# Hybrid DiT backbone with PEER experts, 1 core: the second one-hot of the gate phase is compared by GpSimd ahead of time and comes back from DRAM

## The reference

```python
def peer(h, w_q, subkeys, u, v):                       # per block of 128 tokens
    q = (xb @ w_q).reshape(PEER_BLOCK, PEER_HEADS, 2, PEER_QDIM // 2)
    s = jnp.einsum('thpd,hpkd->thpk', q, subkeys)
    s1, i1 = lax.top_k(s[:, :, 0], PEER_TOPK)          # 16 of 128 keys
    s2, i2 = lax.top_k(s[:, :, 1], PEER_TOPK)
    cand = s1[..., :, None] + s2[..., None, :]
    cidx = i1[..., :, None] * PEER_KEYS + i2[..., None, :]
    sc, pos = lax.top_k(cand, PEER_TOPK)               # 16 experts a head, 8 heads
    idx = jnp.take_along_axis(cidx, pos, axis=-1)
    g = jax.nn.softmax(sc, axis=-1)
    act = jax.nn.gelu(jnp.einsum('thkd,td->thk', u[idx], xb))
    return jnp.einsum('thk,thkd->td', g * act, v[idx])
```

## Time and profile before

| | |
|---|---|
| median of 3 runs | 3708.85 us (3705.79 to 3709.24) |
| span of the profiled execution | 3700.4 us (its own time is not on the page) |
| TensorE busy | 3558.4 us, 96% |
| VectorE busy | 2666.9 us, 72% |
| ScalarE busy | 2003.8 us, 54% |
| GpSimd busy | 139.6 us, 4% |
| moved by DMA | 568.38 MB, mean 154 GB/s |

### The profile page before, as it was taken

How to read it: one execution, slowest core, us unless ns; L and a number is a source line. 1 busy time by engine, 2 the same in 40 slices (tenths; PEclk the granted TensorE clock), 3 DMA queues, 4 the chain that set the end, 5 groups by cost and what they waited for, 6 DMA issues and landing times.

```text
span 3700.4 us, 61292 instructions
## 1 busy us (share of the span) xinstructions
PE 3558.4 (96%) x22710; PEld 3113.8 (84%) x22710; DVE 2666.9 (72%) x5607; ACT 2003.8 (54%) x3922; POOL 139.6 (4%) x134
## 2 busy tenths in 40 slices
PE   7999999999998999999999999999899999979999
PEld 5877787888887899999998888888698888878888
DVE  5447733699868688888767776774765899686666
ACT  3345522566668555555557544434454666684444
POOL 0002000000012000000002000000100000030000
PEclk9999999999999999999999999999999999999999
DMA  5213222455645566566655566633044566605665
GB/s 206 82 67 138 94 97 83 144 183 182 186 151 159 167 187 184 185 186 184 187 184 152 161 186 198 195 119 111 9 164 136 176 187 182 187 29 165 188 190 172
DMA packets 142313, 568.38 MB, mean 154 GB/s; under 512 B 15920, under 2 KB 17456, under 8 KB 130352
## 3 DMA queue, kind: packets, MB, share of 16 engines
q1 hardware_dynamic: 142128, 566.16, 49.0%
HBM read 565.05 MB, written 1.05 MB: 153 GB/s over the span
## 4 chain that ended last, share of the span: by engine, by line
PE 82%; DVE 12%; ACT 3%; issue 2%; DMA 1%; POOL 1%; SPq 0%; DVEq 0%; POOLq 0%; ACTq 0%
PE ps L584 52%; PE ps L1081 13%; PE ps L1099 10%; PE ps L1083 6%; DVE low L1835 3%; DVE arena L1835 3%; ACT arena L1283 2%; DMA ring<-wmod_in 1%; POOL arena L2619 1%; DVE hot_found L1835 1%; DVE arena L2387 1%; DVE arena L2378 1%; DVE ring_low L1835 0%; DVE arena L2380 0%; DVE arena L2375 0%
## 5 line engine op out<-in xcount | busy, mean ns | idle before, releaser
L1283 ACT ACTIVATE high<-ring 128x512 fp32r<-128x512 f32 x1632 | 1028.4, 632 | 1014.7 <-PE ps L584 502.2
L1835 DVE TENSOR_TENSOR low<-ring,high 128x512 fp32r<-128x512 f32 x1632 | 1078.1, 690 | 290.4 <-ACT high L1283 279.4
L584 PE MATMUL ps<-h_pair,high 128*128 128x512 f32 x3456 | 1236.7, 398 | 17.6 <-DVE h_pair L1835 10.3
L584 PE MATMUL ps<-h_pair,low 128*128 128x256 f32 x3456 | 979.7, 283 | 0.0
L584 PEld LDWEIGHTS ps<-h_pair,high 128*128 128x128 f32 x3456 | 653.6, 189 | 171.1 <-issue 11.9
L1081 PE MATMUL ps<-wt,high 128*128 128x512 f32 x2016 | 706.3, 397 | 5.7 <-DVE low L1835 5.7
L584 PEld LDWEIGHTS ps<-h_pair,low 128*128 128x128 f32 x3456 | 655.0, 190 | 0.0
L1083 PE MATMUL ps<-wt,low 128*128 128x256 f32 x2016 | 562.4, 279 | 0.0
L1283 ACT ACTIVATE arena<-ps 128x256 f32<-128x256 f32 (+2 forms) x659 | 274.8, 427 | 382.3 <-PE ps L584 334.0
L1081 PEld LDWEIGHTS ps<-wt,high 128*128 128x128 f32 x2016 | 379.1, 188 | 97.2 <-issue 3.0
L584 PE MATMUL ps<-arena 128*128 128x128 f32 (+7 forms) x2536 | 355.1, 311 | 56.5 <-ACT arena L1283 44.2
(11 more groups left out here) (202 smaller groups left out, 4296.5 us busy)
## 6 DMA issues: line engine op xcount, KB each, us to landing
ring<-u_in SPq DMA_DIRECT2D x384, 512.0 KB, 3.6
ring<-v_in SPq DMA_DIRECT2D x384, 512.0 KB, 3.6
ring<-win_in SPq DMA_DIRECT2D x54, 1024.0 KB, 4.9
ring<-wmod_in SPq DMA_DIRECT2D x24, 1024.0 KB, 5.0
ring<-wq_in SPq DMA_DIRECT2D x48, 512.0 KB, 3.6
ring<-wmod_in SPq DMA_DIRECT2D x48, 512.0 KB, 3.7
ring<-wbr_in SPq DMA_DIRECT2D x16, 768.0 KB, 4.3
ring<-wout_in SPq DMA_DIRECT2D x8, 1024.0 KB, 4.9
```

What stands on the lines that cost most here:

```text
L584: return pe.matmul(o, l_, r, start=first, stop=last)
L1283: return act.activation(o, i_, f, **kw_)
L1835: return dve.tensor_tensor(o, a, b, op)
```

## The change

The second one-hot is no longer compared by VectorE in the gate phase. GpSimd compares it in the u stage, token by token, as soon as the routing result of a half is copied: 32 groups of 8 instructions of 128 x 128, in bfloat16, into four buffers (`hot2_made`). SyncE stores each group to DRAM (`keep_hot2`, 256 KB): groups 0 to 15 after the loads of chunks 66, 68, ... 96, groups 16 to 31 after those of 112 to 127. In the gate phase SyncE loads them back (`bring_hot2`), at most three in flight, into two plus four buffers, of which the four lie over `high`. ScalarE widens from there. Of the eight tokens of a group GpSimd now multiplies six and ScalarE two. `hot2_made` lies over `hot1`, so the first gated copies wait until the last store is done. In layer 1 four chunks of v are loaded between the loads of groups 4 and 5; in layer 0 each modulation chunk is loaded behind a group's one-hot. The second index is copied to float32 (`RT[:, 1]`) where it was bfloat16 (`route2`).

```diff
@@ sync: new functions
+            def keep_hot2(pp, g):
+                sp.wait_ge(*at("ssd_xd", "hot2_made", pp, g))
+                if g:
+                    sp.wait_ge(*at("stored", "hot2", pp, g - 1))
+                sp.dma_start(hot2_kept[pp][g], hot2_made[:, g % 4, :]).then_inc(*inc("stored", "hot2", pp, g, by=16))
+
+            def bring_hot2(pp, g):
+                sp.wait_ge(*at("stored", "hot2", pp, g))
+                if g >= 3:
+                    sp.wait_ge(*at(hot2_loaded(g), "hot2", pp, g - 3))
+                if g >= 6:
+                    sp.wait_ge(*at("hot2", pp, g - 4))
+                elif g >= 2:
+                    sp.wait_ge(cnt.sem("half_free"), 2 * PN["u", pp, CHUNKS - 1] + 2)
+                sp.dma_start(hot2_in(g), hot2_kept[pp][g]).then_inc(*inc(hot2_loaded(g), "hot2", pp, g, by=16))
@@ sync: u stage and gate phase
                         chunk(("u", pp, c))
-                    if l + 1 < DEPTH:
-                        for n in range(2 * MOD_PASS):
-                            chunk(("m", pp, n))
+                        if c in STORE_AT:
+                            keep_hot2(pp, STORE_AT.index(c))
+                    for g in range(5):
+                        bring_hot2(pp, g)
+                    v_ahead = 0 if l + 1 < DEPTH else 4
+                    for c in range(v_ahead):
+                        chunk(("v", pp, c))
+                    for g in range(5, GROUPS):
+                        bring_hot2(pp, g)
+                        if l + 1 < DEPTH and g - 5 < 2 * MOD_PASS:
+                            chunk(("m", pp, g - 5))
@@ scalar: gate_hot1
                     if g >= 2:
                         act.wait_ge(*at("g_product", pp, g - 2))
-                    for j in range(GROUP // 2, GROUP):
+                    else:
+                        act.wait_ge(*at("stored", "hot2", pp, GROUPS - 1))
+                    for j in range(3 * GROUP // 4, GROUP):
...
-                    act.wait_ge(*at("hot2_found", pp, g))
-                    fn(hot2[:, g % 2, :, :].rearrange("p (a b) k -> p a b k", b=2),
-                       hot2_found[:, g % 2, :, :].rearrange("p a (k b) -> p a b k", b=2), ACT.Copy
+                    act.wait_ge(*at(hot2_loaded(g), "hot2", pp, g))
+                    fn(hot2[:, g % 2, :, :].rearrange("p a k -> p (a k)"), hot2_in(g), ACT.Copy
                        ).then_inc(*inc("hot2", pp, g))
@@ vector: gate phase
                         gate_mult(pp, g)
-                        if g + 2 < GROUPS:
-                            one_hot2(pp, g + 2)
@@ gpsimd
-                    pool.wait_ge(*at("route_read", pp, 1))
+                    for g in range(GROUPS):
+                        if g % HALF_GROUPS == 0:
+                            pool.wait_ge(*at("route_read", pp, g // HALF_GROUPS))
+                        if g >= 4:
+                            pool.wait_ge(*at("stored", "hot2", pp, g - 4))
+                        for j in range(GROUP):
+                            i = pool.tensor_scalar(hot2_made[:, g % 4, j * P:(j + 1) * P], iota,
+                                                   RT[:, 1, g * GROUP + j:g * GROUP + j + 1], None, ALU.is_equal)
+                        i.then_inc(*inc("ssd_xd", "hot2_made", pp, g))
+                    pool.wait_ge(*at("stored", "hot2", pp, GROUPS - 1))
...
-                        mult(hot1[:, g % 2, 0:GROUP // 2, :].rearrange("p (a b) k -> p a b k", b=2),
+                        mult(hot1[:, g % 2, 0:3 * GROUP // 4, :].rearrange("p (a b) k -> p a b k", b=2),
```

51 lines of the change are left out of this document (25 added, 26 removed).

## The result

The changed kernel takes 3749.38 us (median of 4 runs, 3743.19 to 3752.66) where the kernel before takes 3709.05 us beside it: ratio 1.0106, 95% interval 1.0091 to 1.0122. It is 1.1% slower; the forecast was 3697 us and the range ended at 3728 us. The profiled execution has a span of 3745.6 us, 45.2 us more than before.

What follows compares the result with a forecast made beforehand. TensorE was taken as the bound, with some 32 us idle in the gate phases, where VectorE and ScalarE set the period. Gate phases -21 and u-alone passes +9 gave -12 us: forecast 3697 us, range 3684 to 3728 us.

Steps and rivals of the forecast that it cites:

- I take 0.25 us, the row that it is nearest to, and keep 0.12 and 0.40 for the range: Stages with u: time of one GpSimd compare of 128 elements, scaled from a multiply of 512 elements in 1.0 us.
- the deadline: Second half of passes with u alone: 51.7 us for 128 compares, 3 to 6 us late, 2 us taken per pass.
- Rival 1: SyncE's wait between loads of chunks 112 to 127: GpSimd too slow, 3722 us at 0.35 us a compare; chance 0.24.
- the free slack: u loads in passes with u alone: needed 8.4 us after issue, so 3.5 us of lateness cost nothing.
- The second cost, VectorE in the ranking: First half of passes with u alone: VectorE's `low` waits for GpSimd's compares, 2.5 us a pass.
- Rival 2: Ranking stages: VectorE becomes the bound, 10 us a pass, with the deadline 3711 us; chance 0.15.
- The stores: Passes with u alone: each 256 KB store lands in 2.3 us, under the chunk period of 2.80 us.
- The gate phases: All three gate phases: -12.7 - 5 - 1.5 - 1.8 = -21 us, bounds -27 and -8 us.
- the ring argument: Third gate phase: GpSimd's multiply and VectorE's compare wait for each other, 1.5 + 0.6 + 0.1 = 2.2 us a group.
- Rival 3: u stages and gate phases: cheap compares, 1 us a pass, loose ring, gate phases at -23, 3687 us; chance 0.18.
- Rival 4: Gate phases: second one-hot's loads come too late, period stays 2.6 us, 3715 us; chance 0.05.

Runs made afterwards that it cites:

- the best kernel here: Against the kernel before: the change with VectorE comparing the second half's groups, GpSimd the first half's, and first-half stores every 2.5 chunks; 3686.28 us, ratio 0.9934.

## Why the prediction was wrong

**The step that failed** is "I take 0.25 us, the row that it is nearest to, and keep 0.12 and 0.40 for the range". A compare takes 0.592 us at its shortest and 0.69 us in the second half. Two things were mis-sized in it. I divided a multiply of 512 elements by four; but a multiply of 128 would already be some 0.4 us by its two sizes (an estimate, 1.04 us less 384 x 1.7 ns), and a compare of 512 elements is itself 1.56 us, not 1.0 us, although it has one streamed input and the multiply two: 2.51 ns an element, where the multiply has (1.47 - 1.04) / 256 = 1.7 ns (128x768 in the fence above, 128x512 in the earlier trace rows). And the 0.27 us of each instruction weigh eight times a group. For both I had a ground in the rows and took it too lightly: that the instruction was another than the one I scaled from ("No row shows one"), and that short instructions carry a fixed part. I bounded the price at 0.40 us, by a fixed part borrowed from VectorE, and ended the range lower still: 3728 us is 0.37 us a compare, and 0.40 us was 3738 us by my own working. With nothing measured of this kind of instruction on GpSimd the upper bound had to be wider, the more so as each 0.01 us beyond the deadline is 1.3 us a pass.

The Trainium skill ("GPSIMD Engine Reference", section "3.1 Elementwise — side-by-side cycle accounting") has 1.03 cycles an element for a body of up to two operations, an estimated 0.11 us for 128 elements. The runs differ: 2.51 ns are three cycles at the 1.2 GHz by which that section turns cycles into time, and the fixed part comes on top. The measurement decides.

**Rival 1's mechanism was right in place and kind, its price too high in one part and too low in the other.** The place is SyncE's wait between the loads of chunks 112 to 127, and the loss is what goes over the deadline: 88.6 - 51.7 - 3.5 (the free slack) = 33.4 us, and 5.9 us from the first half, 39.3 us, against 38.8 us measured. The rival's point, "decides from about 0.32 us a compare", rested on GpSimd having only 28 of the 51.7 us, because it could not run during a VectorE `low`. It ran 128 x 0.597 = 76.4 us of the 88.6 us, 86% (0.597 us is the median of a compare there). By these numbers, and as an estimate, lateness begins at (51.7 + 3.5) / 128 x 0.86 = 0.37 us a compare, where the rival's 28 and 3.5 us give 0.25 us; and it has eaten the gate phases' gain, 29.5 us or 14.75 us a pass, at (51.7 + 3.5 + 14.75) / 128 x 0.86 = 0.47 us. With the measured 0.6 us the rival's own working would have given 76.8 - 28 - 3.5 + 4 = 49 us a pass and some 3786 us, 37 us too much. The price of a compare that it took was too low, the price of VectorE's lock too high. The run with four compares of eight (64 at 0.6 us) is free of loss, the run with six is not.

**The second cost, VectorE in the ranking** (2.5 us a pass), was about right: 1 to 2 us for the narrow compares of the first half, 4 to 6 us with wide ones. Rival 2, which made 10 us of it with compares of 0.25 us, has no run for it, though the compares are more than twice as long.

**The stores** were expected to land in 2.3 us, under the chunk's 2.8 us. They land in 2.2 us only in the second halves of the passes with u alone, where GpSimd holds back the loads; in the first halves the median is 4.5 us, in the pass with u and v 5.0 us, over all 4.4 us. With four compares, where the loads run at full pace in the second half, it is 2.8 us. So the term was too low. In the changed kernel it cost nothing that shows (the run with one compare has the same stores); where VectorE compares ahead it may have.

**The gate phases** were expected at -21 us and give -29.5 us (the run with one compare of eight). Third phase: predicted 2.2 us a group and 12.7 + 0.6 us in all; measured 2.09 us and 94.1 - 77.7 = 16.4 us. First phase: 5.6 us predicted, 10.7 us measured; second 2.1 and 3.8 us. There I counted only half of TensorE's 10 us of idle time, and most of it went: 92.32 of 95 us are busy now. The direction of the ring argument (GpSimd's multiply, then the compare, each shutting the other out) stands, and the split alone in the kernel before shows it from the other side: there it costs 3.9 us in the third phase.

**Rival 3**, a compare of 0.12 to 0.2 us, fell with the price. **Rival 4**, loads too late for the gate phase, fell: ScalarE's widening copy of `hot_later` waits for no transfer in the rows above, at 245 and 257 GB/s in the phases with modulation rows.

Together: -29.5 us in the gate phases and 3749.4 - 3680.4 = 69 us from the compares, 34.5 us for each pass with u alone. By the table it is (403.0 - 365.3) + (403.0 - 365.1) = 75.6 us in the u loads, less 0.8 and 2.1 us, by which a pass that was late ends its gate phase sooner (94.7 for 95.5 us, 75.6 for 77.7 us): 72.7 us. The two ratios, 1.0106 and 0.9913, give 71.6 us. Why a late pass ends its gate phase sooner is not shown.

## What to carry to other kernels

Work moved to an idle engine is free only up to the deadline of whoever waits for it in program order; past it each ns counts by the number of instructions, so price the deadline first (time that is left, divided by the number of instructions) and ask if the unmeasured instruction could exceed it. A duration scaled from another kind of instruction is no bound; where a miss can cost more than twice what the change gains (69 us against 29.5 us here), leave the forecast's range open on that side. Compare stage by stage, from first and last starts of a fixed set of instructions: for the u loads and the gate phases here that repeats to about 1 us where the total scatters by 10. And account for all stages: the kernels in which VectorE compares ahead lose 6 to 8 us in the pass with u and v, where no loss was looked for.

## What was not expected of the hardware

A GpSimd compare with a per-partition value takes 0.27 us and 2.51 ns an element (0.592, 1.556 and 2.838 us for 128, 512 and 1024 elements of float32 to bfloat16), more for each element than a GpSimd multiply of two tensors (1.7 ns); with a constant it takes 0.517 us for 128 (one run). VectorE's compare of 1024 elements with the bfloat16 value takes 0.69 us, seven times less than the eight GpSimd compares of the same group, and this is why the best kernel here gives it the half for which there was least time. A short instruction of GpSimd that is shut out by VectorE, or shuts it out, is much less of a loss in a stage with a full queue than its time suggests: 79 us of compares of 0.6 us beside a VectorE that is busy for 105 of 120 us left TensorE at 120 of 120 us. Compares of 2.8 us were not so harmless (116.91 of 120 us, with GpSimd busy for 49 us).

And a slower TensorE where it had to wait. In the stretch in which GpSimd sets the pace, these windows show the granted clock fall as the idle time grows (windows of the changed kernel, columns as in the earlier trace rows):

```profile
3218.00:3240.00 22.00, 22.00 (x127) 19.31 (x126) 13.87 (x24) 14.69 (x33) 22.00 (x32) 1.00 0.70 215
3240.00:3260.00 20.00, 16.97 (x87) 13.93 (x85) 7.19 (x13) 6.87 (x16) 20.00 (x31) 0.91 0.47 156
3260.00:3280.00 20.00, 14.16 (x60) 11.24 (x61) 7.58 (x13) 6.91 (x16) 20.00 (x30) 0.83 0.44 144
```

These means mix the clock's two levels, 2.4 and 1.2 GHz. In the timeline the matmuls of 128x512 run at 0.39 us behind an idle time of 2.66 us, fall to 0.63 us in the same burst, and are back at 0.39 us after another 0.62 us of idle time:

```profile
3262.11 0.51 PE L623 MATMUL ps<-h_pair,high 128*128 128x512 f32 x1 [2.66 <-DVE low L1876]
...
3262.92 0.39 PE L623 MATMUL ps<-h_pair,high 128*128 128x512 f32 x1
...
3264.39 0.63 PE L623 MATMUL ps<-h_pair,high 128*128 128x512 f32 x1
...
3267.95 0.39 PE L623 MATMUL ps<-h_pair,high 128*128 128x512 f32 x1
```

Over the whole stretch from 3218 to 3300 us a matmul of 128x512 takes 434 ns in the mean where it took 394 ns before (3186 to 3230 us), one of 128x256 302 ns where it took 283. With 162 of each that is an estimated 9.6 us, the 10 us by which TensorE is busier there than its count of matmuls accounts for. It cost little here, since GpSimd, busy for all 82 us, set the pace. What such a fall costs where TensorE is nearly the bound, no run here shows.
